# A hybrid two-layer encoder: two PSUM banks for the projections of the forgetting pairs, and the high halves of weights on ScalarE instead of GpSimd

## What is computed

```python
def forgetting_attention(q, k, v, f_logit):
    ...
    cum = jnp.cumsum(jax.nn.log_sigmoid(f_logit.astype(F32)), axis=1)
    ...
        logits = (jnp.einsum('bqhd,bshd->bhqs', qb.astype(F32), kf) * scale
                  + cq.transpose(0, 2, 1)[..., None] - cum_k[:, :, None, :])
        p = jax.nn.softmax(jnp.where(mask, logits, -jnp.inf), axis=-1)
        return jnp.einsum('bhqs,bshd->bqhd', p, vf)

def mixer_sb_fox(x, w_in, b_f, w_o):
    h = x @ w_in
    ...
    oa = stick_breaking_attention(qa, ka, va).reshape(b, s, -1)
    ob = forgetting_attention(qb, kb, vb, f_logit).reshape(b, s, -1)
    return jnp.concatenate([oa, ob], axis=-1) @ w_o
```

## Time and profile before

| | us |
|---|---|
| median of three runs | 2824.18 |
| lowest, highest run | 2823.06, 2825.07 |
| the profiled execution's own time | 2827.21 |
| its span | 2825.4 |
| PE busy in the span | 2687.5 (95%) |
| DVE, POOL, ACT busy in the span | 1903.7, 1676.1, 1080.0 |

### The profile page before, as it was taken

How to read it: one execution, slowest core, us unless ns; L and a number is a source line. 1 busy time by engine, 2 the same in 40 slices (tenths; PEclk the granted TensorE clock), 3 DMA queues, 4 the chain that set the end, 5 groups by cost and what they waited for, 6 DMA issues and landing times.

```text
span 2825.4 us, 42474 instructions
## 1 busy us (share of the span) xinstructions
PE 2687.5 (95%) x15813; PEld 1363.5 (48%) x16096; DVE 1903.7 (67%) x2637; ACT 1080.0 (38%) x1665; POOL 1676.1 (59%) x916
## 2 busy tenths in 40 slices
PE   7999898899999999999899999899999999999998
PEld 4666554354444444444444444456654444444443
DVE  6788778575666674256999999688847656664043
ACT  3566566243333210014554343666643433331000
POOL 4777656336676679845347777711113666675884
PEclk9999999999999999999999999999999999999999
DMA  4122455631111253332213222488873111113332
GB/s 150 50 64 72 90 119 119 193 115 60 58 53 55 68 179 127 105 132 83 53 38 142 111 79 100 114 183 185 185 208 132 68 60 60 60 54 126 127 105 97
DMA packets 299309, 294.82 MB, mean 104 GB/s; under 512 B 239408, under 2 KB 239536, under 8 KB 299168
## 3 DMA queue, kind: packets, MB, share of 16 engines
q1 hardware_dynamic: 287360, 268.90, 33.1%
q10 hardware_dynamic: 11808, 23.99, 2.6%
HBM read 189.51 MB, written 35.70 MB: 80 GB/s over the span
## 4 chain that ended last, share of the span: by engine, by line
PE 78%; DVE 6%; issue 5%; ACT 4%; DMA 4%; POOL 2%; ACTq 1%; POOLq 0%; DVEq 0%; SPq 0%
PE ps L1691 23%; PE ps L334 20%; PE ps L316 14%; PE ps L650 4%; PE ps L2529 4%; PE ps L399 4%; DMA pt<-split 3%; PE ps L920 2%; PE ps L2019 2%; PE ps L656 1%; PE ps L2063 1%; DVE split L848 1%; PE ps L2557 1%; PE ps L891 1%; DVE prob L1035 1%
## 5 line engine op out<-in xcount | busy, mean ns | idle before, releaser
L273 POOL TENSOR_TENSOR w_hi<-w_stage,ones 128x1024 bf16<-128x1024 f32 (+1 forms) x115 | 238.5, 2074 | 138.1 <-PE ps L334 85.3
L276 POOL TENSOR_TENSOR w_lo<-w_stage,w_hi 128x1024 bf16<-128x1024 f32 (+1 forms) x115 | 265.2, 2306 | 9.0
L1508 DVE SCALAR_TENSOR_TENSOR x_res<-x_res,ps 128x1024 f32<-128x1024 f32 x32 | 39.0, 1218 | 319.6 <-PE ps L334 318.8
L334 PE MATMUL ps<-w_hi,hid_hi 128*128 128x512 bf16 x689 | 206.4, 379 | 1.6 <-POOL w_lo L276 0.8
L334 PE MATMUL ps<-w_hi,hid_lo 128*128 128x512 bf16 x690 | 206.5, 379 | 0.7
L334 PE MATMUL ps<-w_lo,hid_hi 128*128 128x512 bf16 x690 | 206.4, 379 | 0.7
L2529 PE MATMUL ps<-lat_hi,q_now 128*128 128x512 bf16 (+3 forms) x736 | 185.9, 326 | 7.6 <-DVE row_max L2616 6.8
L316 PE MATMUL ps<-xt_hi,w_hi 128*128 128x512 bf16 x598 | 179.2, 380 | 3.1 <-DVE score L2178 2.5
L316 PE MATMUL ps<-xt_hi,w_lo 128*128 128x512 bf16 x596 | 179.0, 380 | 0.8 <-issue 0.2
L316 PE MATMUL ps<-xt_lo,w_hi 128*128 128x512 bf16 x592 | 178.1, 380 | 0.8
L1691 PE MATMUL ps<-xt_lo,w_hi 128*128 128x512 bf16 x426 | 161.5, 379 | 0.5
(11 more groups left out here) (309 smaller groups left out, 7507.6 us busy)
## 6 DMA issues: line engine op xcount, KB each, us to landing
w_stage<-in_l_up SPq DMA_DIRECT2D x88, 512.0 KB, 3.8
w_stage<-in_l_down SPq DMA_DIRECT2D x88, 512.0 KB, 3.7
w_stage<-in_l_o SPq DMA_DIRECT2D x32, 512.0 KB, 6.2
w_stage<-in_l_q SPq DMA_DIRECT2D x32, 512.0 KB, 5.1
q_split<-q_out SPq DMA_DIRECT2D x32, 512.0 KB, 2.6
q_now<-q_split SPq DMA_DIRECT2D x16, 1024.0 KB, 5.7
w_stage<-in_l_qkv SPq DMA_DIRECT2D x24, 512.0 KB, 4.1
x_spilled<-x_res ACTq DMA_DIRECT2D x16, 512.0 KB, 2.6
```

Of the source, the lines that this page charges most:

```text
L273: pool.tensor_tensor(hi, w_stage[slot][:, 0:cols], ones[:, 0:1].to_broadcast([P, cols]), ALU.mult).then_inc(w_cast[slot], 1)
L276: pool.tensor_tensor(lo, w_stage[slot][:, 0:cols], hi, ALU.subtract).then_inc(w_split[slot], 1)
L334: mm = pe.matmul(ps[:, bank + h, :], a[:, k, rows], w[:, h * HALF:(h + 1) * HALF], start=(k == first and m == 0), stop=(k == tiles - 1 and ...
```

## The change

It has two parts. First, in the forgetting pairs the halves of the projection alternate between PSUM banks 5 and 4: `proj_bank` gives even halves bank 5 and odd ones bank 4, and a half waits only for the evacuation of the half two before it. In pair 4, the first one, bank 5 still belongs to the last stick-breaking pair at the start; there halves 0 and 1 both use bank 4 as before, and half 2 waits for the last use of bank 5 (`turning.lo`). Second, the high halves of the 15 strips and row tiles that are split during pairs 4 to 7 are made by ACT, as the last instruction of a slot (`fox_weights_hi`); POOL keeps the low halves. The slots are tabled in the new function; the row tiles of pair 7 move from POOL's steps 1, 3, 5, 7 and 9 to slots 3, 4, 6, 9 and 11. ACT's program for pairs 5 and 6, a loop before, is written out. The loads stay where they are in SP's program.

```diff
-        def proj_bank(e, pair):
-
-            return 2 + e if isinstance(pair, int) and pair == 0 else 4
+        def proj_bank(e, pair, kind=None, prev=None):
+
+            if isinstance(pair, int) and pair == 0:
+                return 2 + e
+            return 5 if kind == "fox" and e % 2 == 0 and (prev == "fox" or e > 0) else 4
...
                     if isinstance(pair, int) and pair == 1 and e == 0:
                         pe.wait_ge(s_pjl, 3)
+                    elif kind == "fox" and prev == "sb" and e == 2:
+                        pe.wait_ge(turning.lo, BATCHES * FIRST_FOX)
+                    elif kind == "fox" and (prev == "fox" or e > 2):
+                        pe.wait_ge(s_pjl, 6 * pair + e - 1)
                     elif not first:
                         pe.wait_ge(s_pjl, 6 * pair + e)
...
                     act.activation(take[t % 4][:, 0:n], banks(2 * (t % 2))[:, 0:n], ACT.Exp, scale=SB_SCALE,
                                    bias=neg_max[:, t % 4:t % 4 + 1],
                                    accum_out=row_sum[:, t % 4:t % 4 + 1]).then_inc(s_sfree, 1)
+                    fox_weights_hi(act, pair, slot)
...
+        def fox_weights_hi(act, pair, slot):
+
+            qkv = {2: (2, pair + 1), 6: (0, pair + 2), 11: (1, pair + 2)}
+            outputs = {7: 3, 8: 0, 12: 1} if pair == N_PAIRS - 2 else {3: 2, 4: 4, 6: 5, 9: 6, 11: 7}
+            if slot in qkv and qkv[slot][1] < N_PAIRS:
+                n, of = qkv[slot]
+                act.wait_ge(w_loaded[n], 16 * (feed_qkv.use(n, of) + 1))
+                act.wait_ge(s_pj, 6 * (of - 1) + 2 * (n + 1))
+                act.activation(w_hi[n][:, :], w_stage[n][:, :], ACT.Copy).then_inc(w_cast[n], 1)
+            elif pair >= N_PAIRS - 2 and slot in outputs:
+                n = outputs[slot]
+                act.wait_ge(w_loaded[feed_o0.slot(n)], 16 * (feed_o0.use(n, 0) + 1))
+                if n != 3:
+                    act.wait_ge(s_pj, 6 * (N_PAIRS - 1) + 2 * (n + 1) if n < 2 else 6 * N_PAIRS)
+                act.activation(held(feed_o0, n)[0], w_stage[feed_o0.slot(n)][:, 0:D_MODEL],
+                               ACT.Copy).then_inc(w_cast[feed_o0.slot(n)], 1)
+
+        def output_lo(pool, n):
+            slot = feed_o0.slot(n)
+            hi, lo = held(feed_o0, n)
+            pool.wait_ge(w_cast[slot], feed_o0.use(n, 0) + 1)
+            pool.tensor_tensor(lo, w_stage[slot][:, 0:D_MODEL], hi, ALU.subtract).then_inc(w_split[slot], 1)
...
             def splits_o(t):
-                if t == 1:
-                    pool.wait_ge(s_pj, 6 * N_PAIRS)
-                ahead = {1: 2, 3: 4, 5: 5, 7: 6, 9: 7}
+                ahead = {3: 2, 4: 4, 6: 5, 9: 6, 11: 7}
                 if t in ahead:
-                    split_piece(pool, feed_o0, ahead[t], 0)
+                    output_lo(pool, ahead[t])
```

More of the change, by code:

```diff
@@ L628, in program, with proj_half @@
         half_slots = [(0, 1), (2, 3, 4), (5, 6, 7), (8, 9), (10, 11, 12), (13, 14, 15)]
-        def proj_bank(e, pair):
-            return 2 + e if isinstance(pair, int) and pair == 0 else 4
-        def proj_half(pe, e, pair, units):
-            n, bank = e // 2, proj_bank(e, pair)
+        def proj_bank(e, pair, kind=None, prev=None):
+            if isinstance(pair, int) and pair == 0:
+                return 2 + e
+            return 5 if kind == "fox" and e % 2 == 0 and (prev == "fox" or e > 0) else 4
+        def proj_half(pe, e, pair, units, kind=None, prev=None):
+            n, bank = e // 2, proj_bank(e, pair, kind, prev)
             first = isinstance(pair, int) and pair == 0
@@ L664, in opens_half, with proj_slot @@
             return any(slots[0] == slot for slots in half_slots)
-        def proj_slot(pe, slot, pair):
+        def proj_slot(pe, slot, pair, kind, prev):
             for e, slots in enumerate(half_slots):
@@ L669, in proj_slot @@
                     at, of = slots.index(slot), len(slots)
-                    proj_half(pe, e, pair, range((8 * at + of - 1) // of, (8 * at + 8 + of - 1) // of))
+                    proj_half(pe, e, pair, range((8 * at + of - 1) // of, (8 * at + 8 + of - 1) // of), kind, prev)
         def proj_ends(slot, pair, project, first):
@@ L676, in proj_ends, with proj_dst @@
             return [(e, pair + 1) for e, slots in enumerate(half_slots) if project and slots[-1] + 1 == slot]
-        def proj_dst(e, pair):
+        def proj_dst(e, pair, kind, prev):
             if e < 4:
@@ L696, in proj_evac_hi, with proj_evac_lo @@
             act.activation(hi, src, ACT.Copy).then_inc(s_pjh, 1)
-        def proj_evac_lo(dve, e, pair):
-            hi, lo, src = proj_dst(e, pair)
+        def proj_evac_lo(dve, e, pair, kind=None, prev=None):
+            hi, lo, src = proj_dst(e, pair, kind, prev)
             dve.wait_ge(s_pjh, 6 * pair + e + 1)
@@ L896, in pair_tensor @@
                     if project and not opens_half(slot):
-                        proj_slot(pe, slot, pair + 1)
+                        proj_slot(pe, slot, pair + 1, kind, prev)
                     if not project:
@@ L1179, in splits @@
                 def splits(t):
[L1180 to L1182 removed]
+                    if t == 3:
                         split_qkv_lo(pool, 2, pair + 1)
[L1184 to L1185 removed]
                     elif t in (7, 12):
@@ L1233, in heads_scalar @@
                 make_current_v(act, hh, 0)
-            all_pairs(act, pair_scalar)
+            first_fox = N_SB // 2
+            pair_scalar(act, 0, "sb", None, True)
+            with act.Fori(1, first_fox - 1) as pair:
+                pair_scalar(act, pair, "sb", "sb", True)
+            pair_scalar(act, first_fox - 1, "sb", "sb", True)
+            pair_scalar(act, first_fox, "fox", "sb", True)
+            for pair in range(first_fox + 1, N_PAIRS - 1):
+                pair_scalar(act, pair, "fox", "fox", True)
+            pair_scalar(act, N_PAIRS - 1, "fox", "fox", False)
+            pair_scalar(act, N_PAIRS, None, "fox", False)
         def heads_vector(dve):
```

26 lines of the change are left out of this document (9 added, 17 removed).

## The result

The changed kernel takes 2830.26 us (median of 22 runs, 2828.38 to 2833.26); the kernel before, in runs made beside these, 2825.24 us (22 runs, 2823.06 to 2827.61). The ratio is 1.0016, interval 1.0011 to 1.0022: 5.0 us slower, 0.16 to 0.18%, clear of zero but under the 0.2% that the prediction set as its bound; the interval reaches 0.22%, a little over it.

The account below looks back on a forecast made before the run. DVE was taken to bound first halves of pairs 4 to 6, level with PE in second halves. -0.3 + 0.2 - 1.4 + 0.3 + 2.7 = +1.5 us gave 2825.7, range 2817 to 2832.

Parts of the forecast that it names:

- its own signs: Profile: nq_lo/nv_lo waits gone, mix_lo waits grown, 640-wide split 0.87 us, ACT waits 2.6 and 3.0, pair 7's end 2.7 later.
- Two banks, value 0: Pairs 4 to 6: 8.39 us of PE waits go but return as mix_lo waits; bounds 0 and -8.39.
- the rival in which PE sets the pace: Pairs 4 to 6: the 8.39 us are kept, so -5.7 us, 2818.5; chance 0.20.
- First halves, -0.3, +0.2, -1.4: Pairs 4, 5, 6, in us: DVE splits freed of POOL gain 2.13, less delays from low halves and casts.
- Second halves, +0.15, +0.15 and 0: Pairs 4, 5, 6, in us: slot 11's cast delays slot 10's high half; pair 6 about 0; +0.3 in all.
- Pair 7, +2.7: Pair 7's end: ACT's waits for o6 and o7 loads delay the value product 2.7 us; bounds -2.4 and +6.2.
- forecast -1.5: Start of pair 7: splits of slots 0 and 1, freed of POOL, gain 1.5 us by slot 8.
- it counts whole: After pair 7: PE's chain runs to the end without another DVE wait, so all +2.7 us reach the total.
- The slower one: Pair 7: ACT's load waits and two casts count whole, 7.7 us, less 1.2 earlier: +6.5, 2830.7 us; chance 0.20.
- The loads did not come in time: Rival claiming o6 and o7 land before their casts in pair 7: sum -3.6, 2820.6 us; chance 0.10.

Follow-up runs that it names:

- the banks alone: Kernel before plus only the two alternating PSUM banks, high halves still on POOL: 2831.24 against 2826.19 us, ratio 1.0018.
- PE kept busy: Kernel before plus the two banks and unused matmuls, eight before slot 8's and four before slot 0's value products: 2827.03 against 2826.78 us, ratio 1.0002.
- the casts alone: Kernel before plus only the high halves moved to ACT, all projection halves in bank 4: 2829.31 us, ratio 1.0013.
- the chosen parts: Kernel before plus ACT high halves only for slot 6's strip (at slot 8), o3, o0, o2, o4, o5; bank 4: 2819.47 against 2826.78 us.
- the sixteen matmuls: Unused 512-column matmuls before the value product after pair 7, added to the kernel with few ACT high halves in bank 4: 2821.23 us, ratio 0.9980.
- o6 and o7 on POOL: Changed kernel with the high halves of o6 and o7 back on POOL: 2827.40 against 2826.19 us, ratio 1.0009.

## Why the prediction was right, and where its sum was short

The forecast was 2825.7 us and no change beyond 0.2%; it became 2830.26 and +0.16 to 0.18%. Its sum was +1.5 us and should have been +5.0. That the time still came out as no change is partly luck: against the median of three runs from which the prediction started, 2824.18, it would be 6.1 us, over the bound of 5.65. Of its own signs, the six waits are gone, the waits for `mix_lo` have grown, PE's waits in all did not fall, and ACT's two waits are there but did not reach the end undiminished.

**Two banks, value 0.** The waits went and were given back, as forecast: slot 8 at +0.01 and +0.15 us with the banks alone, and that run refutes the rival in which PE sets the pace. The Trainium skill's hint ("Perfetto Trace Analysis", "Optimization Strategy"), by which repeated gaps may ask for another buffer, bore no fruit here: the gaps ended, and the time rose by 5.05 us. The step that failed is the upper end of its bounds, 0. Two short waits (1.48 and 1.65 us) became one long one (2.77), and in some executions PE's clock fell at a longer wait: +5.05 us with the banks alone, +0.3 with PE kept busy. The rows for it were there: the 5.24 us of the value product behind the wait of 5.14. I had read that wait as a wait, and not asked why sixteen matmuls behind it took 5.24 us where six took 1.47.

**First halves, -0.3, +0.2, -1.4.** The changed kernel's table gives -0.28, +1.09 - 0.94 = +0.15, and +2.24 - 3.68 = -1.44. DVE's timeline in pair 5 shows the gains and the loss that cancels them:

```profile
371.20 0.88 DVE L854 SCALAR_TENSOR_TENSOR split<-take,row_inv,split 128x640 bf16<-128x640 f32 x1
...
373.00 0.75 DVE L854 SCALAR_TENSOR_TENSOR split<-take,row_inv,split 128x512 bf16<-128x512 f32 x1 [0.34 <-ACT split L849]
...
375.65 2.08 DVE L854 SCALAR_TENSOR_TENSOR split<-take,row_inv,split 128x384 bf16<-128x384 f32 x1 [0.46 <-ACT split L849]
```

The 640-wide split fell from 2.14 to 0.88 us (0.87 forecast) and the 512-wide to 0.75, while the 384-wide one rose from 0.62 to 2.08, a loss of 1.46 where I took 0.95. Against that, ACT's cast held the high half before it up by 0.3 us where I took 0.65, and the 896-wide split of slot 1 took 1.84 us, 0.69 over the 1.15 of before, where I took 0.73; so part of the close sum is errors that cancel. The 384-wide split starts inside POOL's low half:

```profile
375.19 2.12 POOL L1056 TENSOR_TENSOR w_lo<-w_stage,w_hi 128x1024 bf16<-128x1024 f32 x1 [4.39 <-ACT w_hi L1066]
```

and ends at 377.73, 0.42 us after it. The Trainium skill ("SBUF — State Buffer", "Who interferes with whom") has the rule: a DVE instruction with two inputs in SBUF and a GpSimd instruction that reads SBUF contend for a shared read port, and the order of issue decides which of them is blocked. These rows agree.

**Second halves, +0.15, +0.15 and 0.** Measured (without the clock) from slot 9 to the next slot 0: +0.94 - 1.41 = -0.47, +3.68 - 2.77 = +0.91, +3.34 - 2.24 = +1.10, in all +1.5 where I had +0.3. For o1's cast at slot 12 of pair 6 I had charged nothing. From slot 8 of pair 6 to slot 0 of pair 7 the casts alone lose 1.43 us (-0.27 to +1.16) and the chosen parts, which leave o1 on POOL, 0.80 (-3.82 to -3.02), which speaks for some 0.6 us for that cast, though the two kernels differ in more than it. Pair 5's +0.91 is not shown to be the casts': with the banks and matmuls but no cast it is +1.30 (+0.18 to +1.48), and the chosen parts without and with the sixteen matmuls, the same program up to there, differ by 1.3 us at pair 6's slot 0 (-2.35 and -1.07), where PE waits for the transposing DMA 0.92 us in one and 2.26 in the other.

**Pair 7, +2.7.** Until slot 8 -1.72 (forecast -1.5). Then ACT's casts of o6 and o7 wait for their loads, as ACT's timeline shows:

```profile
493.98 1.06 ACT L1072 ACTIVATE xt_hi<-w_stage 128x1024 bf16<-128x1024 f32 x1 [2.66 <-DMA w_stage<-in_l_o]
...
505.37 1.06 ACT L1072 ACTIVATE xt_hi<-w_stage 128x1024 bf16<-128x1024 f32 x1 [3.88 <-DMA w_stage<-in_l_o]
```

2.66 us against 2.6, and 3.88 against 3.0. The split of slot 8, behind which o7's load is issued, ended 3.3 us behind o6's cast, nearly as forecast (3.2), but by luck: nothing stood between its two halves, where I took 0.8 us, and it took 2.21 us instead of 1.27, because the low half of o6 on POOL ran beside it. What made the wait longer is mostly the load itself. SP's timeline has its issue, before:

```profile
494.44 0.93 SPq L248 DMA_DIRECT2D w_stage<-in_l_o  x1
```

and now:

```profile
500.37 0.93 SPq L248 DMA_DIRECT2D w_stage<-in_l_o  x1
```

It landed at 498.82 before, 4.4 us later, and now at 505.3, 5.0 us later; why is open. The split of slot 8, on DVE's timeline:

```profile
496.10 2.21 DVE L854 SCALAR_TENSOR_TENSOR split<-take,row_inv,split 128x1024 bf16<-128x1024 f32 x1 [2.54 <-ACT split L849]
```

To the end of pair 7 that makes +4.71, with the start -1.72 + 4.71 = +3.0 against +2.7. PE's clock is low there too (from 498.4 to 505.2 and from 508.6 on), but has no part in it: the chain of work that ended last runs from slot 8 to the value product at 515.79 through DVE, ACT, SP and the loads of o6 and o7, and holds no matmul. I said that it counts whole from there; 0.76 us came back in the value product, whose clock was low in both kernels, but for 3.1 us here and for 4.6 before.

**The rivals.** The slower one gave 2830.7, nearly what was measured, for a reason that did not hold: it had ACT's two waits and casts count whole, 7.7 us; they were 6.5 + 2 x 1.06 = 8.7 and counted 4.7. Its sum also left out the 1.5 us that the start of pair 7 gains. The loads did not come in time either: o6 landed 493.98 - 488.48 = 5.5 us after slot 6's split (5.44 before).

In the profiled execution the sum is then three clock falls of 1.7 us, 5.05; first halves -1.57; second halves +1.54; pair 7 +2.99 - 0.76: +7.25, as the table has it. Why the medians have only +5.0 was not taken apart. The mean granted clock does not say that the changed kernel's falls are rarer over many executions: it is 0.991 in its 22 runs and in the profiled one. That of the kernel before is 0.992 in the runs beside the experiments and 0.993 in its profiled execution, so that execution may have had fewer falls than most.

## What to carry to other kernels

Before a wait is taken away, ask where PE will wait instead and for how long in one piece: several short waits can be cheaper than one long one, because the matmuls behind it can run at the lower clock. When work moves from an engine that had time to wait for a load (POOL stood 11.22 us) to one on the path, leave the piece whose load is late where it is, or move the load first, which no run here tried. And place a GpSimd instruction by what DVE starts meanwhile: in the first half of pair 5 casts at slots 2 and 6 made +0.15 us, while a cast at slot 8, with the strip of slot 2 left whole on POOL, made -1.47.

## What the runs showed of the hardware that I had not expected

From pair 4 to slot 0 of pair 7 PE stood idle for 2.0 to 2.9 us in one piece 33 times in the fourteen profiled executions. At 11 of these waits, of 2.12 to 2.79 us, its clock fell, and that cost 0.9 to 2.9 us, mostly 1.7; at none of the shorter ones did it, the 1.65 us among them. So it does not fall each time. The kernel with o6 and o7 on POOL is up to there the same program as the changed one, and its PE timeline at pair 4's slot 8 has the same wait, 2.78 us against 2.79, but six matmuls at 1.45 us against 1.87:

```profile
323.57 1.45 PE L926 MATMUL ps<-turned,v_both 128*128 128x512 bf16 x6 [2.78 <-DVE mix_lo L1031]
```

In the changed kernel itself a wait of this length, at pair 6's slot 0, was not followed by a fall:

```profile
407.34 1.47 PE L926 MATMUL ps<-turned,v_both 128*128 128x512 bf16 x6 [2.81 <-DMA turned<-split]
```

So one profile is not enough to count such falls; the mean granted clock of the runs (0.9896 with the banks alone, 0.9924 with PE kept busy) tells more. And sixteen matmuls that compute nothing, put into a wait of 5.14 us, took 2.3 us off the work behind it.
